# A key-choosing stage whose weight preparation moves from GpSimd to VectorE

## The chip, the core and the metric

The kernel runs on one core of one Trainium2 chip. The metric is the device time of one execution in microseconds (us). A core has five engines that work from queues of their own: TensorE (PE in the profile, its weight loads PEld), VectorE (DVE), ScalarE (ACT), GpSimd (POOL) and SyncE (SP, which here only issues transfers). They wait for each other through semaphores.

## The reference, cut to what matters

The program is two blocks of a network over 512 tokens of width 1024. The first block has four mixers; one of them attends only to chosen keys. Its choice, and the gated sum into which each mixer's result goes, are

```python
rel = jax.nn.relu(jnp.einsum('bqhd,bsd->bqhs', iqb, ik).astype(jnp.float32) * IDX_DIM ** -0.5)
score = jnp.einsum('bqhs,bqh->bqs', rel, iwb.astype(jnp.float32)) * IDX_HEADS ** -0.5
score = jnp.where(admissible[None], score, -jnp.inf)
_, idx = lax.top_k(score, keep)          # keep = 128 of 512
...
gates = jax.nn.sigmoid(p["gate"].reshape(bsz, seq, N_BRANCHES, D_MODEL))
merged = jnp.sum(gates * jnp.einsum('bsnc,ncd->bsnd', ys, w_branch[l]), axis=2)
```

## The kernel before, in words

The kernel is a row of stages, each a block with a barrier at its end: the next stage's first instructions start when every engine has finished the last one. Through most stages runs one *stream* of weight tiles (class `Stream`): while an engine works on the stage's own algorithm, the others push tiles of the big products through in between. A tile is 128 columns of a weight matrix, 128 x 1024 values in SBUF. It passes through these steps:

- SyncE loads it (`raw`, three slots of two tiles, `Stream.load`).
- ScalarE rounds it to the high half, `w_hi` (L1406, `Stream.round`). It may do so two tiles ahead: `w_hi` and `w_lo` have two buffers each.
- `Stream.rest` makes the low half, `w_lo = raw - w_hi` (L1430, one instruction over 128 x 1024 values). It counts up the semaphore `split`, for which TensorE waits.
- TensorE makes 24 matmuls into `acc` (L1476 to L1478), and, where the tile belongs to a gated sum, 4 more into `br` (L1486).
- ScalarE takes `tanh` of `acc` into `sg` (L1417), VectorE multiplies `sg` by `br` (L1439, `Stream.product`, semaphore `mixed`), and `Stream.sum` adds `sg` to `merged`, or copies it there where it is the first mixer's (L1448, semaphore `added`).

There is one buffer `br` only. So TensorE's four L1486 matmuls of a tile wait until the tile before has had its product. The waits of the other steps are the same in all stages:

```python
def dve(self, dve, n):
    if n == 0:
        self.rest(dve, self.nc.vector, 0)
    self.rest(dve, self.nc.vector, n + 1)
    if n:
        self.mix(dve, n - 1)        # product, then sum, both on VectorE
```

All stages but one call this `Stream.dve`. The exception is `selection_stage`. It streams nine tiles, `fill` (below f0 to f8): the eight of the first gated sum and the first one of the second. VectorE there searches the 128 largest scores of each of 128 queries, for three blocks of queries (i = 1, 2, 3, with 256, 384 and 512 keys). A block has

- a sum of eight heads: one L2324 and seven L2326 (`masks = rel * iw + masks`),
- 16 rounds, each a MAX8 (L2341) that finds the eight largest and a MATCH_REPLACE8 (L2342, with a short MATCH_VALUE_LOAD ahead of it) that takes them out,
- one L2344 that turns the result into a mask.

After every sixth of the 48 rounds, and once at the end, stands a *step* of the stream: steps 0 to 7 stand ahead of rounds 0, 6, 12, ... 42, step 8 behind the last round. In step s VectorE makes the product of tile f(s-1) (none in step 0, whose tile before has no gated sum). GpSimd meanwhile runs a loop of its own over the same nine tiles, `Stream.pool`: the low half of tile f(s+1) as soon as ScalarE has rounded it, then the sum of tile f(s-1) once its product is there. The order of each engine's work is the order in which the code issues it; no planner is in between.

Of the kernel before, what the change touches and what calls it, by code (L numbers as in the profile page):

```python
# [1031 lines left out]
def experts_by_token(c, table, x_dram, y_dram, w_gate, w_up, w_down, room_yg, room):  # L1032
# [5 lines left out]
    with ExitStack() as ctx:  # L1038
# [17 lines left out]
        with c.stage() as block:  # L1056
# [11 lines left out]

            @block.gpsimd
            def _(pool):  # L1070
                def index(dst, j, col, count):
                    nc.gpsimd.tensor_copy(dst, table[:, j, col:col + 1]).then_inc(idx_copied, 1)
# [239 lines left out]
class Stream:  # L1312
# [148 lines left out]
        if n:  # L1461
            self.mix(dve, n - 1)

    def pool(self, pool, n):
        self.rest(pool, self.nc.gpsimd, n + 1)
        self.sum(pool, self.nc.gpsimd, n - 1)

    def pe(self, pe, n):
        tile = self.tiles[n]
        pe.wait_ge(self.split, n + 1)  # L1470
# [756 lines left out]
def selection_stage(c, stream, fill, iq, small, ik, gain, lat, lat_t, iw, masks):  # L2227

    nc = c.nc
    with ExitStack() as ctx:
        rel, best = c.sb(ctx, "rel", [P, 8, S]), c.sb(ctx, "best", [P, 8])
        rows, sq, st = c.sb(ctx, "rows", [P, NT, P]), c.sb(ctx, "sq", [P, NT, 64]), c.sb(ctx, "st", [P, 3, NT, 1])
        ps, tps = c.ps(ctx, "rel_ps", [P, 4, 512]), c.ps(ctx, "turn_ps", [P, 512])
        ik_in, turned, rows_ready, var, rooted, lat_ready, dots, relu, used, chain = (c.sem(x) for x in (
            "ik_in", "turned", "rows", "var", "rooted", "lat", "dots", "relu", "used", "dve"))
        rounds, per = 3 * KEEP // 8, 6
        with c.stage() as block:
            @block.sync  # L2240
            def _(sp):
                for b in range(4):
                    sp.dma_start(ik[32 * b:32 * b + 32, :], small[64:96, :]).then_inc(ik_in, 16)
                for n in fill:
                    stream.load(sp, n + 2)

            @block.tensor
            def _(pe):
                def products(i):
                    pe.wait_ge(ik_in, 64)  # L2250
                    for h in range(8):
                        n = 8 * (i - 1) + h
                        if n >= 4:
                            pe.wait_ge(relu, n - 3)
                        b, wd = 32 * (h % 4), (i + 1) * P
                        pe.matmul(ps[:, n % 4, 0:wd], iq[b:b + 32, h // 4, i * P:(i + 1) * P], ik[b:b + 32, 0:wd],
                                  start=True, stop=True).then_inc(dots, 1)

                for i in range(NT):
                    mm = pe.transpose(tps[:, i * P:i * P + 120], small[0:120, i * P:(i + 1) * P], c.const("ident")[0:120, 0:120])  # L2260
                mm.then_inc(turned, 1)
                for s, n in enumerate(fill):
                    if s == 0:
                        products(1)
                    if s == 1:
                        products(2)
                    if s == 4:
                        products(3)
                    stream.pe(pe, n)
                    if s == 1:  # L2270
                        pe.wait_ge(lat_ready, 1)
                        for i in range(NT):
                            mm = pe.transpose(tps[:, i * P:(i + 1) * P], lat[:, i, :], c.const("ident"))
                        mm.then_inc(turned, 1)

            @block.scalar
            def _(act):
                def rectified(i):
                    for h in range(8):
                        n, wd = 8 * (i - 1) + h, (i + 1) * P  # L2280
                        act.wait_ge(dots, n + 1)
                        if n >= 8:
                            act.wait_ge(used, n - 7)
                        nc.scalar.activation(rel[:, h, 0:wd], ps[:, n % 4, 0:wd], ACT.Relu, scale=32 ** -0.5).then_inc(relu, 1)

                act.wait_ge(turned, 1)
                nc.scalar.copy(rows[:, :, 0:120], tps[:].rearrange("p (i d) -> p i d", i=NT)[:, :, 0:120]).then_inc(rows_ready, 1)
                for s, n in enumerate(fill):
                    stream.act(act, n)
                    if s == 0:  # L2290
                        rectified(1)
                        act.wait_ge(var, 1)
                        nc.scalar.activation(st[:, 1], st[:, 0], ACT.Sqrt).then_inc(rooted, 1)
                    if s == 1:
                        rectified(2)
                    if s == 2:
                        act.wait_ge(turned, 2)
                        nc.scalar.copy(lat_t, tps[:])
                    if s == 4:
                        rectified(3)  # L2300

            @block.gpsimd
            def _(pool):
                for n in fill:
                    stream.pool(pool, n)

            @block.vector
            def _(dve):
                run = Chain(dve, chain)
                dve.wait_ge(rows_ready, 1)  # L2310
                run(nc.vector.tensor_tensor(sq[:], rows[:, :, 0:64], rows[:, :, 0:64], ALU.mult))
                run(nc.vector.tensor_reduce(st[:, 0], sq[:], AX.X, ALU.add))
                run(nc.vector.tensor_scalar(st[:, 0], st[:, 0], 1.0 / 64, 1e-6, ALU.mult, ALU.add))
                dve.sem_inc(var, 1)
                run(nc.vector.tensor_scalar(iw, rows[:, :, 112:120], 8 ** -0.5, None, ALU.mult))
                taken = 0
                for i in range(1, NT):
                    wd = (i + 1) * P
                    m, d = masks[:, i - 1, 0:wd], masks[:, i - 1, i * P:wd]
                    for h in range(8):  # L2320
                        n = 8 * (i - 1) + h
                        dve.wait_ge(relu, n + 1)
                        if h == 0:
                            ins = nc.vector.tensor_scalar(m, rel[:, h, 0:wd], iw[:, i, 0:1], None, ALU.mult)  # L2324
                        else:
                            ins = nc.vector.scalar_tensor_tensor(m, rel[:, h, 0:wd], iw[:, i, h:h + 1], m, ALU.mult, ALU.add)  # L2326
                        ins.then_inc(used, 1)
                        dve.wait_ge(used, n + 1)
                    run(nc.vector.tensor_tensor(d, d, c.const("causal"), ALU.add))
                    if i == 1:  # L2330
                        dve.wait_ge(rooted, 1)
                        run(nc.vector.reciprocal(st[:, 2], st[:, 1]))
                        run(nc.vector.tensor_tensor(sq[:], rows[:, :, 0:64], st[:, 2].broadcast_to([P, NT, 64]), ALU.mult))
                        for r in range(2):
                            run(nc.vector.tensor_tensor(lat[:, :, 64 * r:64 * r + 64], sq[:],
                                                        gain.unsqueeze(1).broadcast_to([P, NT, 64]), ALU.mult))
                        dve.sem_inc(lat_ready, 1)
                    for _r in range(KEEP // 8):
                        if taken % per == 0:
                            stream.product(dve, fill[taken // per] - 1)  # L2340
                        run(nc.vector.max(best[:], m))  # L2341
                        run(nc.vector.match_replace(m, best[:], m, TAKEN))  # L2342
                        taken += 1
                    run(nc.vector.tensor_scalar(m, m, TAKEN / 1.5, NEG, ALU.is_ge, ALU.mult))  # L2344
                for n in fill[(rounds + per - 1) // per:]:
                    stream.product(dve, n - 1)


def gla_stage(c, stream, fill, q, k, vt, low, gate, a_up, a_bias, gain, lat, w_uv, th, y_lat, y):
# [489 lines left out]
```

## Time and profile before

| what | value |
|---|---|
| median of three runs | 2821.92 us (2821.71 to 2823.41) |
| the profiled execution, device time | 2821.36 us |
| its span, first to last instruction | 2819.6 us |
| PE, PEld, DVE, ACT, POOL busy | 2266.8, 1693.7, 1423.7, 854.0, 125.6 us |
| L1430 on DVE, all stages | x203, 248.0 us, mean 1224 ns |

In the tables of the profile a row names line, engine, operation and `output<-input`, then the shape of output and input. A busy time is the sum of instruction times on an engine. Instructions of one engine overlap a little: the next can start some hundredths of a microsecond before the last is through, so what an instruction costs in a row of them is the distance from its start to the next start. PEclk is the clock granted to TensorE as a share of its full speed: 1.00 is 2.4 GHz and 0.50 is 1.2 GHz.

### The profile page before, as it was taken

The page shows a single profiled execution, that of the slowest core. Times are in us where ns is not written, and L with a number is a line of the kernel's source. Part 1 is how long each engine was busy: PE and PEld are TensorE (multiplying, and loading weights), DVE is VectorE, ACT ScalarE, POOL GpSimd, SP SyncE. Part 2 cuts the span into 40 slices and gives each one's busy share as a digit, 9 for nine tenths or more (in the row PEclk, how much of TensorE's full clock was granted, in tenths as well). Part 3 has the DMA queues.
Part 4 walks back from the last instruction along what each step waited for, and adds up shares of the span by engine and source line. Part 5 has one row for each costly group of instructions (what it writes and reads, how often), then busy time and mean ns, then how long its engine had stood idle before and what let it go on. Part 6 is the DMA issues. An engine that isn't in the chain of part 4 may idle for free. (4 is left out here: it accounts for less than half of the span.)

```text
span 2819.6 us, 30685 instructions
## 1 busy us (share of the span) xinstructions
PE 2266.8 (80%) x11238; PEld 1693.7 (60%) x11238; DVE 1423.7 (50%) x2420; ACT 854.0 (30%) x1395; POOL 125.6 (4%) x161
## 2 busy tenths in 40 slices
PE   6345599899985299994259998999964998999986
PEld 4145476566764166763247766777754776687765
DVE  2272335866434266664434457584333445767333
ACT  2020133223221166652233323222222433232221
POOL 0000000200000122221000000000000000000000
PEclk9655599999996599997579999999987999999998
DMA  4100233122110599994233221223114331122311
GB/s 125 64 12 8 79 97 96 56 79 72 60 60 18 148 335 334 341 338 151 101 123 113 75 71 53 75 94 120 41 67 136 97 90 50 59 85 95 118 53 67
DMA packets 281413, 300.03 MB, mean 106 GB/s; under 512 B 58958, under 2 KB 253598, under 8 KB 281226
## 3 DMA queue, kind: packets, MB, share of 16 engines
q1 hardware_dynamic: 271786, 289.57, 31.9%
q0 software_dynamic: 9472, 8.43, 0.9%
q8 instruction: 94, 1.54, 0.2%
q14 instruction: 61, 0.49, 0.1%
HBM read 294.89 MB, written 33.19 MB: 116 GB/s over the span
## 5 line engine op out<-in xcount | busy, mean ns | idle before, releaser
L1476 PE MATMUL acc<-x_hi,w_hi 128*128 128x512 f32 x1632 | 679.7, 416 | 37.5 <-DVE w_lo L1430 32.5
L1478 PE MATMUL acc<-x_hi,w_lo 128*128 128x512 f32 x1632 | 644.3, 395 | 0.0
L1477 PE MATMUL acc<-x_lo,w_hi 128*128 128x512 f32 x1632 | 644.3, 395 | 0.0
L1406 ACT CAST w_hi<-raw 128x1024 fp32r<-128x1024 f32 x212 | 220.8, 1044 | 767.5 <-PE acc L1478 711.7
L1430 DVE TENSOR_TENSOR w_lo<-raw,w_hi 128x1024 fp32r<-128x1024 f32 x203 | 248.0, 1224 | 394.0 <-ACT w_hi L1406 389.9
L1476 PEld LDWEIGHTS acc<-x_hi,w_hi 128*128 128x128 f32 x1632 | 312.5, 192 | 123.5 <-DVE w_lo L1430 33.5
L1477 PEld LDWEIGHTS acc<-x_lo,w_hi 128*128 128x128 f32 x1632 | 312.3, 191 | 75.2 <-issue 13.9
L1478 PEld LDWEIGHTS acc<-x_hi,w_lo 128*128 128x128 f32 x1632 | 311.2, 191 | 68.5
L1486 PE MATMUL br<-y_t,raw_b 128*128 128x512 f32 x448 | 215.8, 605 | 20.2 <-DVE sg L1439 20.2
L1224 DVE TENSOR_TENSOR w_lo<-wgu,w_hi 128x1024 fp32r<-128x1024 f32 x128 | 151.1, 1220 | 117.8 <-ACT w_hi L1180 113.3
L1180 ACT CAST w_hi<-wgu 128x1024 fp32r<-128x1024 f32 x128 | 128.6, 1050 | 158.6 <-DMA wgu<-in_moe_w_up 152.2
L1486 PEld LDWEIGHTS br<-y_t,raw_b 128*128 128x128 f32 x448 | 85.2, 192 | 87.0 <-issue 78.9
L1143 PE MATMUL ps<-wd,y 128*128 128x512 f32 x256 | 115.3, 593 | 0.5 <-DVE y L1244 0.5
L1130 PE MATMUL ps<-w_hi,x_hi 128*128 128x512 f32 x256 | 103.8, 405 | 2.7 <-DVE x_lo L1218 1.7
L692 PE MATMUL ps<-w_hi,m_hi 128*128 128x512 f32 x192 | 77.8, 405 | 35.0 <-DVE w_lo L708 35.0
L1132 PE MATMUL ps<-w_hi,x_lo 128*128 128x512 f32 x256 | 101.2, 395 | 0.0
L1131 PE MATMUL ps<-w_lo,x_hi 128*128 128x512 f32 x256 | 100.8, 394 | 0.0
L1439 DVE SCALAR_TENSOR_TENSOR sg<-sg,br 128x512 f32<-128x512 f32 x112 | 76.4, 682 | 39.9 <-PE br L1486 36.7
L2131 DVE SCALAR_TENSOR_TENSOR y_t<-pad,w,y_t 128x512 f32<-128x512 f32 x120 | 90.1, 751 | 3.4
L1612 ACT ACTIVATE probs<-scores,stat 128x256 f32<-128x256 f32 (+3 forms) x96 | 51.8, 540 | 124.9 <-DVE stat L1573 124.9
L1621 ACT COPY probs_t<-t_ps 128x256 f32<-128x256 f32 (+3 forms) x96 | 38.9, 406 | 142.1 <-PE t_ps L1534 142.1
L1417 ACT ACTIVATE sg<-acc 128x512 f32<-128x512 f32 x112 | 66.2, 591 | 36.7 <-PE acc L1478 36.6
(486 smaller groups left out, 2877.3 us busy)
## 6 DMA issues: line engine op xcount, KB each, us to landing
raw<-in_w_in SPq DMA_DIRECT2D x61, 1024.0 KB, 5.5
raw<-in_w_gate SPq DMA_DIRECT2D x40, 1024.0 KB, 5.2
wgu<-in_moe_w_gate SPq DMA_DIRECT2D x32, 1024.0 KB, 10.2
wgu<-in_moe_w_up SPq DMA_DIRECT2D x32, 1024.0 KB, 13.3
wd<-in_moe_w_down SPq DMA_DIRECT2D x32, 1024.0 KB
raw_b<-in_w_branch SPq DMA_DIRECT2D x56, 256.0 KB, 2.8
y_t<-in_w_out SPq DMA_DIRECT2D x6, 2048.0 KB, 7.9
room<-in_x SPq DMA_DIRECT2D x2, 2048.0 KB, 8.5
```

What stands on the lines that cost most here:

```text
L1130: pe.matmul(ps[:, 0, :], x_hi[:, u, k, :], w_hi[:, k, :], start=(k == 0), stop=False)
L1131: pe.matmul(ps[:, 0, :], x_hi[:, u, k, :], w_lo[:, k, :], start=False, stop=False)
L1132: mm = pe.matmul(ps[:, 0, :], x_lo[:, u, k, :], w_hi[:, k, :], start=False, stop=(k == KT - 1))
L1143: mm = pe.matmul(ps[:, 1 + 2 * u + half, :], ht[:, u, m * P:(m + 1) * P], wd[:, j % SLOTS, m, half * 512:half * 512 + 512], start=(m == 0) ...
L1180: nc.scalar.copy(part(w_hi, p), part(wgu[:, j % SLOTS], p)).then_inc(w_rounded, 1)
L1224: nc.vector.tensor_tensor(part(w_lo, p), part(wgu[:, j % SLOTS], p), part(w_hi, p).bitcast(F32), ALU.subtract).then_inc(w_split, 1)
L1406: self.nc.scalar.copy(self.w_hi[:, n % 2], self.weights(n)).then_inc(self.rounded, 1)
L1430: eng.tensor_tensor(self.w_lo[:, n % 2], self.weights(n), self.w_hi[:, n % 2].bitcast(F32), ALU.subtract).then_inc(self.split, 1)
L1476: pe.matmul(acc, hi, tile.hi[:, k, :], start=(k == 0), stop=False)
L1477: pe.matmul(acc, hi, tile.lo[:, k, :], start=False, stop=False)
L1478: mm = pe.matmul(acc, lo, tile.hi[:, k, :], start=False, stop=(k == KT - 1))
L1486: mm = pe.matmul(self.br[:], self.raw_b[:, b % self.SLOTS, k, tile.at:tile.at + P], tile.row[:, k, :], start=(k == 0), stop=(k == 1))
```

## The change

`Stream.pool` and the GpSimd loop are gone. At each of the nine steps VectorE calls `Stream.dve`, which makes the low half of the next tile, the product of the last one, and its sum. What an engine other than these two does, and in which order, stays as it was.

```diff
-    def pool(self, pool, n):
-        self.rest(pool, self.nc.gpsimd, n + 1)
-        self.sum(pool, self.nc.gpsimd, n - 1)
...
-            @block.gpsimd
-            def _(pool):
-                for n in fill:
-                    stream.pool(pool, n)
...
                     for _r in range(KEEP // 8):
                         if taken % per == 0:
-                            stream.product(dve, fill[taken // per] - 1)
+                            stream.dve(dve, fill[taken // per])
                         run(nc.vector.max(best[:], m))
                         run(nc.vector.match_replace(m, best[:], m, TAKEN))
...
                 for n in fill[(rounds + per - 1) // per:]:
-                    stream.product(dve, n - 1)
+                    stream.dve(dve, n)
```

VectorE around step 1, between rounds 5 and 6 of the search, before (`sg` is the gate of a tile, `br` its mixer's product, `best` the eight largest of a round):

```order
L2342 MATCH_REPLACE masks<-best,masks 128x256
L2341 MAX best<-masks 128x8
L2342 MATCH_REPLACE masks<-best,masks 128x256
L1439 SCALAR_TENSOR_TENSOR sg<-sg,br 128x512
L2341 MAX best<-masks 128x8
L2342 MATCH_REPLACE masks<-best,masks 128x256
```

The same place on VectorE now (lines behind the removed ones have moved up by 4 to 10):

```order
L2332 MATCH_REPLACE masks<-best,masks 128x256
L2331 MAX best<-masks 128x8
L2332 MATCH_REPLACE masks<-best,masks 128x256
L1430 TENSOR_TENSOR w_lo<-raw,w_hi 128x1024
L1439 SCALAR_TENSOR_TENSOR sg<-sg,br 128x512
L1448 COPY merged<-sg 128x512
L2331 MAX best<-masks 128x8
L2332 MATCH_REPLACE masks<-best,masks 128x256
```

The low half of the next tile now stands ahead of the product, and the sum behind it. Step 0 has the low half alone.

VectorE at the end of the stage, before:

```order
L2341 MAX best<-masks 128x8
L2342 MATCH_REPLACE masks<-best,masks 128x512
L2344 TENSOR_SCALAR masks<-masks 128x512
L1439 SCALAR_TENSOR_TENSOR sg<-sg,br 128x512
L152 UNCONDITIONAL_BRANCH
L1699 UNCONDITIONAL_BRANCH
L1564 SCALAR_TENSOR_TENSOR scores<-s_ps,bias 128x128
```

And now, where the branch at L152 is again the stage's end:

```order
L2331 MAX best<-masks 128x8
L2332 MATCH_REPLACE masks<-best,masks 128x512
L2334 TENSOR_SCALAR masks<-masks 128x512
L1430 TENSOR_TENSOR w_lo<-raw,w_hi 128x1024
L1439 SCALAR_TENSOR_TENSOR sg<-sg,br 128x512
L1448 COPY merged<-sg 128x512
L152 UNCONDITIONAL_BRANCH
L1695 UNCONDITIONAL_BRANCH
L1560 SCALAR_TENSOR_TENSOR scores<-s_ps,bias 128x128
```

In step 8 too, the last product, for which TensorE's last four matmuls of the stage wait, has the low half of the next stage's first tile ahead of it.

## Rows read from the trace of the kernel before

**Rows 1.** The selection stage as one stretch: busy time of each engine.
```profile
479.40:580.10 100.70, 81.45 (x309) 55.12 (x308) 86.76 (x191) 27.31 (x47) 26.69 (x17) 0.90 0.18 55
```
**Rows 2.** Waits, 479 to 582 us: who waited for whom, total, times, longest.
```profile
PE br L1486 <- DVE sg L1439: 13.0, 3, 7.8
```
**Rows 3.** Groups of GpSimd, 479 to 582 us: busy us, mean ns, idle before.
```profile
L1430 POOL TENSOR_TENSOR w_lo<-raw,w_hi 128x1024 fp32r<-128x1024 f32 x9 | 21.9, 2436 | 515.4 <-ACT w_hi L1406 515.4
L1448 POOL COPY merged<-sg 128x512 f32<-128x512 f32 x8 | 4.9, 614 | 35.9 <-DVE sg L1439 35.9
```
**Rows 4.** Timeline of DVE in another stage: start us, duration us, instruction.
```profile
1621.22 1.22 DVE L1430 TENSOR_TENSOR w_lo<-raw,w_hi 128x1024 fp32r<-128x1024 f32 x1 [0.87 <-ACT w_hi L1406]
1622.36 0.68 DVE L1439 SCALAR_TENSOR_TENSOR sg<-sg,br 128x512 f32<-128x512 f32 x1
1623.08 0.43 DVE L1448 COPY merged<-sg 128x512 f32<-128x512 f32 x1
1623.42 0.42 DVE L1567 TENSOR_SCALAR scores<-s_ps 128x256 f32<-128x256 f32 x1
```
**Rows 5.** Timelines of DVE and ACT at the steps of the stage.
```profile
498.35 0.69 DVE L1439 SCALAR_TENSOR_TENSOR sg<-sg,br 128x512 f32<-128x512 f32 x1 [0.72 <-DVE masks L2342]
498.96 0.42 DVE L2341 MAX8 best<-masks 128x8 f32<-128x256 f32 x1
...
506.50 1.04 ACT L1406 CAST w_hi<-raw 128x1024 fp32r<-128x1024 f32 x1 [5.18 <-PE acc L1478]
508.27 0.69 DVE L1439 SCALAR_TENSOR_TENSOR sg<-sg,br 128x512 f32<-128x512 f32 x1 [3.45 <-PE br L1486]
...
566.87 0.69 DVE L1439 SCALAR_TENSOR_TENSOR sg<-sg,br 128x512 f32<-128x512 f32 x1
577.04 0.69 DVE L1439 SCALAR_TENSOR_TENSOR sg<-sg,br 128x512 f32<-128x512 f32 x1
```
**Rows 6.** L2326 in blocks 2 and 3: ns min/median/max; GpSimd's timeline at both places.
```profile
L2326 DVE SCALAR_TENSOR_TENSOR masks<-rel,iw,masks x7: 618/619/2635, 513.6 to 519.5; 128x384 f32<-128x384 f32 x7
515.27 2.50 POOL L1430 TENSOR_TENSOR w_lo<-raw,w_hi 128x1024 fp32r<-128x1024 f32 x1 [4.68 <-ACT w_hi L1406]
...
L2326 DVE SCALAR_TENSOR_TENSOR masks<-rel,iw,masks x7: 750/752/2774, 543.2 to 550.0; 128x512 f32<-128x512 f32 x7
544.21 2.82 POOL L1430 TENSOR_TENSOR w_lo<-raw,w_hi 128x1024 fp32r<-128x1024 f32 x1 [3.62 <-ACT w_hi L1406]
```
**Rows 7.** L2342 in blocks 1 and 3: ns min/median/max, first and last start.
```profile
L2342 DVE MATCH_REPLACE8 masks<-best,masks x16: 406/408/411, 492.3 to 512.4; 128x256 f32<-128x256 f32 x16
...
L2342 DVE MATCH_REPLACE8 masks<-best,masks x16: 675/676/680, 551.9 to 575.9; 128x512 f32<-128x512 f32 x16
```
**Rows 8.** Timeline of PE in the stage, at its end, and once later.
```profile
558.00 3.75 PE L1486 MATMUL br<-y_t,raw_b 128*128 128x512 f32 x4 [7.80 <-DVE sg L1439]
...
567.88 1.88 PE L1486 MATMUL br<-y_t,raw_b 128*128 128x512 f32 x4
569.19 0.80 PE L1476 MATMUL acc<-x_hi,w_hi 128*128 128x512 f32 x1
...
577.87 1.95 PE L1486 MATMUL br<-y_t,raw_b 128*128 128x512 f32 x4 [2.63 <-DVE sg L1439]
580.15 0.38 PE L1526 MATMUL s_ps<-lat_t,proj 64*128 64x128 f32 x2 [0.32 <-PEq L152]
...
2396.73 3.43 PE L1486 MATMUL br<-y_t,raw_b 128*128 128x512 f32 x4 [3.78 <-DVE sg L1439]
```
**Rows 9.** Stretches: length, busy PE, PEld, DVE, ACT, POOL; PEclk, DMA share, GB/s.
```profile
553.00:556.00 3.00, 0.00 (x0) 0.00 (x0) 2.86 (x7) 0.00 (x0) 0.00 (x0) 0.52 0.00 0
577.00:579.00 2.00, 1.13 (x3) 0.68 (x4) 0.69 (x2) 0.00 (x0) 0.61 (x1) 1.00 0.00 0
602.00:604.00 2.00, 2.00 (x6) 1.61 (x5) 1.95 (x3) 0.63 (x2) 0.00 (x0) 0.50 0.00 0
630.00:632.00 2.00, 2.00 (x7) 1.56 (x6) 1.93 (x4) 0.00 (x0) 0.00 (x0) 0.60 0.00 0
```

## The prediction

> **What bounds the kernel now.** I read the stage's stretch first, then who waited for whom in it, then GpSimd's groups, and last the timelines of VectorE and TensorE around the steps. The stretch from 479.4 to 580.1 us is the selection stage. VectorE is busy in 86.76 of its 100.70 us, TensorE in 81.45, GpSimd in 26.69 [rows 1]. The reader should see that VectorE is the limit, and that its real load is above 86.76: each round waits for the one before, and the small gaps of that count as idle. TensorE waits three times, 13.0 us in all, for VectorE's product L1439 [rows 2], and its last four matmuls start at 577.87, just after VectorE's last product ended at 577.04 + 0.69 = 577.73 [rows 5, 8]. The next stage's first matmul starts at 580.15, with a branch ahead of it [rows 8]: the barrier. So what VectorE adds ahead of its last product goes one for one into the time, less what VectorE now waits itself. GpSimd's 26.8 us of work [rows 3] are nowhere on that path.
>
> **The change part by part.**
>
> *Low halves and sums on VectorE.* The trace has this very triple on VectorE in another stage: L1430, L1439, L1448 start at 1621.22, 1622.36 and 1623.08, and the next instruction at 1623.42 [rows 4]. So a low half costs 1.14 us, and product and sum 0.72 + 0.34 = 1.06. A product alone costs 498.96 - 498.35 = 0.61 [rows 5]. A step thus grows by 1.14 ahead of its product, and by 1.06 - 0.61 = 0.45 from the product to the next round. Up to the last product there are 9 low halves and 7 sums: 9 x 1.14 + 7 x 0.45 = 10.26 + 3.15 = 13.41 us. The eighth sum, 0.45, stands behind the last product and beside TensorE's last four matmuls, so it costs nothing; were they gone it would cost its 0.45.
>
> *Waits of VectorE that take some of it.* In step 1 VectorE waited 0.72 us; in step 2, 3.45 us for TensorE's `br` [rows 5]. Both waits come early, when VectorE is less than one tile behind. Step 0 adds 1.14. Step 1's wait vanishes whole: the product moves from 498.35 by 1.14 + 1.14 - 0.72 = 1.56, the next round by 2.01. In step 2 the rounds ended at 508.27 - 3.45 = 504.82; now at 506.83. The low half needs ScalarE's rounding, over at 506.50 + 1.04 = 507.54, hence starts about 507.6, and the product follows at 508.75, against 508.27: 0.48 late. From then on `br` and the rounded tile are always there first. So 0.72 + (3.45 - 0.77) = 3.40 us are absorbed.
>
> *GpSimd's work gone from beside VectorE.* Of the seven L2326 of block 2 one takes 2635 ns where the median is 619, in block 3 one takes 2774 against 752. GpSimd has a low half there at 515.27 for 2.50 us and at 544.21 for 2.82 us, within both chains [rows 6]. No other of the 14 is long. I take both stalls as collisions that go with GpSimd's work: 2.02 + 2.02 = 4.04 us back, all on VectorE's chain. The bounds are 0 (the stalls have another cause) and, if half of the other GpSimd low halves cost VectorE something unseen, a little more; I take 4.04, since both rows show it. The rounds show nothing of the kind: L2342 stays within 406 to 411 ns in block 1 and 675 to 680 in block 3 [rows 7], though GpSimd worked beside them in both.
>
> Here the Trainium skill can be weighed ("SBUF — State Buffer", section "Who interferes with whom"): a VectorE instruction with two SBUF inputs excludes a GpSimd instruction that reads SBUF, and the loser stands still for the whole instruction. L2326 reads `rel` and `masks`, and fits. MATCH_REPLACE8 is written with two inputs as well, `best` and `masks`, and by a plain reading it should collide too, and the sum would turn into a gain of some 4 us (rival D). The trace does not agree: no L2342 is long.
>
> *Sum at the last product.* 13.41 - 3.40 - 4.04 = 5.97 us: it starts at 583.01, TensorE's last four matmuls at 577.87 + 5.97 = 583.84.
>
> *TensorE's clock at the stage's end.* In step 7 the product moves by 5.97 - 1.14 - 0.45 = 4.38, from 566.87 to 571.25 [rows 5], so it ends at 571.94. Tile f7's `br` matmuls started at 567.88 and f8's main matmuls 1.31 later, and these ended at 577.87 - 2.63 = 575.24, 6.05 after their start at 569.19 [rows 8]. Now they run from some 573.3 to 579.3, and TensorE is idle for 4.5 us until 583.84, where it was idle for 2.63. After 2.63 the clock stood at 1.00 [rows 9]. In the idle stretch of 7.80 it had fallen to 0.50 from about its fourth microsecond, and after it the four matmuls took 3.75 us, not 1.95; after an idle stretch of 3.78 us later in the kernel they took 3.43 [rows 8, 9]. With 4.5 I expect the slow clock. It costs at least 3.43 - 1.95 = 1.5 us, which the barrier passes on, and up to 2.6 if, as after 558.0, the clock stays at half for about 5.3 us of work. I take 2.0; the other end is 0 (clock kept).
>
> *What costs nothing.* The low half of f(s+1) is now made late in steps 1 to 7, but TensorE needs it only after `br` of f(s), which itself waits for the product of the same step; so it is always there first. The loads that wait for `split` start up to 13 us later, but with three slots each is wanted two groups (four tiles, over 28 us) later. GpSimd has nothing left in the stage and nobody waits for it.
>
> Sum: 5.97 + 2.0 = 8.0 us. Against the profiled execution that is 2821.36 + 8.0 = 2829.3; the median of the runs is 0.56 above it, so 2829.9.
>
> **The rivals.**
>
> *A. The clock is kept at the stage's end.* Everything else as above: +6.0, 2827.9 us. For it: the clock held through 2.63 us. Against: it had fallen after 3.78.
>
> *B. The slow L2326 are not GpSimd's doing.* Then 4.04 us do not come back, and the stage ends 10.0 us late, with the slow clock 12: 2831.9 to 2833.9 us. Against it is that both lie exactly under a GpSimd low half. A run of worse clocks in the next stage (below, in the other direction) would look alike in the total.
>
> *C. Not slower: the clock pays it back in the next stage.* That stage loses its clock twice for a few microseconds, PEclk 0.50 in 602 to 604 and 0.60 in 630 to 632 [rows 9], in the short idle moments of its attention units. Where the clock falls depends on how idle moments lie, and the shift moves them. A cold stretch of about 3.5 us costs 1.7 us of TensorE's time. If both vanish, 3.4 us come back; with the clock kept at the stage's end too, 6.0 - 3.4 = +2.6 remain: 2824.5 us, no measurable change. It decides from one of the two gone together with the clock kept: +4.3. Likewise two further cold stretches would give +11.4.
>
> *D. Faster: the rounds too were held up by GpSimd.* Six of its nine low halves lie beside rounds; at 2.02 us each, as in L2326, 12 us more come back: 8.0 - 12.1 = -4, 2817.8 us. Rows 7 speak plainly against it.
>
> **How the numbers follow.** About 0.2%, or 5.6 us, can be told from no change. Forecast (slow clock, 4.04 back) 0.50; A 0.27; B, or a worse clock later, 0.10; C 0.11; D and anything else that gains 0.02. Slower by over 0.2% (above 2827.6) holds nearly all of the forecast and B, and some 0.6 of A: 0.49 + 0.16 + 0.10 = 0.75; same 0.22, of A's lower part, C and a little of the forecast; faster 0.03. The range leaves out most of C, the top of B and D: 2826.0 to 2833.5.
>
> **What the profile will show.** VectorE should have 9 L1430 of about 1.23 us and 8 L1448 of 0.43 in the stage, and no GpSimd row there. No L2326 over 0.76 us. No wait ahead of step 1's product, and under 1 us ahead of step 2's low half. Products of steps 3 to 8 late by 0.0, 1.6, 3.2, 2.8, 4.4 and 6.0 us, the next stage's first matmul near 586.1 to 588. TensorE's wait before its last four matmuls near 4.5 us, with PEclk 0.50 behind it. I am wrong if an L2326 is still long, if VectorE waits in a late step, or if the next stage does not start later by what VectorE's last product is late.

## The result: 5.9 us slower, with the profile after

The changed kernel takes 2829.28 us, the median of 11 runs (2828.14 to 2833.34); the kernel before, over its own 11 runs, 2823.36 us (2821.41 to 2827.67). The ratio is 1.0023, 95% interval 1.0013 to 1.0032, that is 3.7 to 9.0 us slower. The profiled execution took 2830.9 us, its span 2829.1.

The selection stage after, as one stretch (length, busy PE, PEld, DVE, ACT, POOL, then PEclk, DMA share, GB/s; it answers to [rows 1]):

```profile
480.86:589.50 108.64, 84.08 (x309) 56.03 (x308) 94.46 (x208) 27.42 (x47) 0.00 (x0) 0.89 0.17 51
```

It is 7.94 us longer (100.70 before), VectorE is busy 7.70 us more, and GpSimd not at all. The stage also begins 1.45 us later than in the first profile, before anything that the change touches; six profiles of the two kernels place its first VectorE instruction anywhere from 481.29 to 483.70 us. I therefore count all times inside the stage from that instruction (481.29 us before, 482.74 after). From the next stage's first matmul to the span's end it is 2239.45 us before and 2239.55 after: in this pair of profiles nothing is given back or lost later. Between executions this remainder moves more: over all six profiles, three of each kernel, it lies between 2236.2 and 2239.6 us, with a mean of 2238.0 before and 2238.2 after.

The groups of VectorE in the stage (busy us, mean ns, idle before; to [rows 3, 6]):

```profile
L1430 DVE TENSOR_TENSOR w_lo<-raw,w_hi 128x1024 fp32r<-128x1024 f32 x9 | 11.0, 1225 | 1.6 <-ACT w_hi L1406 1.2 <-DVE lat L2325 0.2
...
L2316 DVE SCALAR_TENSOR_TENSOR masks<-rel,iw,masks 128x512 f32<-128x512 f32 x7 | 5.3, 752 | 0.2
...
L2316 DVE SCALAR_TENSOR_TENSOR masks<-rel,iw,masks 128x384 f32<-128x384 f32 x7 | 4.3, 619 | 0.2
L1448 DVE COPY merged<-sg 128x512 f32<-128x512 f32 x8 | 3.4, 427 | 0.3
```

The nine low halves and eight sums are there, 14.4 us busy. The head sums now have means of 619 and 752 ns, the old medians: both long ones are gone. Step 2 on VectorE's timeline, to [rows 4, 5]:

```profile
508.04 0.41 DVE L2332 MATCH_REPLACE8 masks<-best,masks 128x256 f32<-128x256 f32 x1
509.70 1.22 DVE L1430 TENSOR_TENSOR w_lo<-raw,w_hi 128x1024 fp32r<-128x1024 f32 x1 [1.25 <-ACT w_hi L1406]
510.84 0.68 DVE L1439 SCALAR_TENSOR_TENSOR sg<-sg,br 128x512 f32<-128x512 f32 x1
511.55 0.43 DVE L1448 COPY merged<-sg 128x512 f32<-128x512 f32 x1
511.90 0.42 DVE L2331 MAX8 best<-masks 128x8 f32<-128x256 f32 x1
```

The distances 1.14, 0.71 and 0.35 are those of the other stage. The wait of 1.25 us is for ScalarE's rounding; `br` is there when the product's turn comes. TensorE and VectorE at the stage's end (to [rows 5, 8]):

```profile
583.97 1.23 DVE L1430 TENSOR_TENSOR w_lo<-raw,w_hi 128x1024 fp32r<-128x1024 f32 x1
585.12 0.68 DVE L1439 SCALAR_TENSOR_TENSOR sg<-sg,br 128x512 f32<-128x512 f32 x1
```

```profile
585.94 3.29 PE L1482 MATMUL br<-y_t,raw_b 128*128 128x512 f32 x4 [4.32 <-DVE sg L1439]
589.55 0.61 PE L1522 MATMUL s_ps<-lat_t,proj 64*128 64x128 f32 x4 [0.32 <-PEq L152]
```

The last product starts at 585.12 - 482.74 = 102.38 us of the stage, before at 577.04 - 481.29 = 95.75: 6.63 later. The next stage's first matmul is at 106.81 against 98.86: 7.95 later. The clock around the last four matmuls (stretches as in [rows 9]):

```profile
583.00:586.00 3.00, 0.06 (x1) 0.09 (x1) 2.90 (x5) 0.00 (x0) 0.00 (x0) 1.00 0.00 0
586.00:588.00 2.00, 2.00 (x3) 0.88 (x4) 0.26 (x1) 0.00 (x0) 0.00 (x0) 0.60 0.00 0
```

Through most of the idle stretch of 4.32 us the clock still stands at 2.4 GHz, and it falls to 1.2 GHz just as the matmuls run: 3.29 us for the four, 1.95 before.

### The profile page after: what moved, and what is told of

It is laid out like the page before. It is cut to its first block and busy times, and to the rows that moved or that the text cites. A ratio compares the mean times of both kernels' runs of the same rounds, so it can differ in the third digit from the quotient of the medians.

```text
span 2829.1 us, 30691 instructions
## 1 busy us (share of the span) xinstructions
PE 2272.9 (80%) x11238; PEld 1697.7 (60%) x11238; DVE 1431.7 (51%) x2437; ACT 853.3 (30%) x1395; POOL 100.0 (4%) x144
## 5 line engine op out<-in xcount | busy, mean ns | idle before, releaser
L1430 DVE TENSOR_TENSOR w_lo<-raw,w_hi 128x1024 fp32r<-128x1024 f32 x212 | 259.0, 1224 | 394.8 <-ACT w_hi L1406 391.1
L1118 PE MATMUL ps<-consts,y 128*128 128x128 f32 x256 | 34.1, 277 | 54.2 <-DMA y<-x_scratch,gi 54.2
```

Of the source, the lines that this page charges most:

```text
L1430: eng.tensor_tensor(self.w_lo[:, n % 2], self.weights(n), self.w_hi[:, n % 2].bitcast(F32), ALU.subtract).then_inc(self.split, 1)
```

## The experiments

All of them change only the selection stage. The table counts in us from the stage's first VectorE instruction; "four" is the duration of TensorE's last four matmuls of the stage.

| kernel | last product | four | next stage's first matmul | runs |
|---|---|---|---|---|
| before, three profiles | 95.75, 96.16, 95.97 | 1.95, 3.43, 1.95 | 98.86, 100.75, 99.08 | 2823.36 |
| changed, three profiles | 102.38, 102.23, 101.82 | 3.29, 3.38, 3.59 | 106.81, 106.77, 106.56 | 2829.28 |
| low halves only | 99.24 | 3.35 | 103.74 | 2825.28 (1 run) |
| sums only | 101.25 | 2.89 | 105.30 | 2829.61 (1 run) |
| GpSimd waits | 92.02 | 3.65 | 96.82 | 2818.20 |
| product first | 101.49 | 3.22 | 105.86 | 2827.81 (1 run) |
| GpSimd work beside | 104.25 | 3.75 | 109.15 | 2833.94 (1 run) |
| TensorE kept busy | 102.25 | 1.96 | 105.36 | 2825.81 |
| waits, early product | 87.28 | 1.88 | 93.40 | 2816.17 |

### The two halves of the change, each alone

```diff
     def pool(self, pool, n):
-        self.rest(pool, self.nc.gpsimd, n + 1)
         self.sum(pool, self.nc.gpsimd, n - 1)
...
+                            stream.rest(dve, nc.vector, fill[taken // per] + 1)
                             stream.product(dve, fill[taken // per] - 1)
...
+                    stream.rest(dve, nc.vector, n + 1)
                     stream.product(dve, n - 1)
```

> VectorE makes the low halves in the nine steps, GpSimd keeps the sums. My theory adds its terms one by one: nine low halves of 1.14 us, less 3.4 us of VectorE's early waits (2.8 where the slow clock at the stage's start lasts as long as in the changed kernel), less 4.04 us for the two collisions, since GpSimd makes no low half any more: VectorE's last product 2.8 to 3.5 us later than before, counted from the stage's first VectorE instruction. No L2316-like head sum above 0.76 us. Rival (the two long head sums are not GpSimd's low halves' doing): they stay, and the product is 6.9 to 7.5 us late.

Measured: last product at 99.24, 3.49 us later than in the first profile of before, at the upper end of my interval, and 3.28 later than the mean of before's three; no long head sum (blocks of seven in 4.54 and 5.48 us, against 6.56 and 7.50). The rival fell.

The other half keeps GpSimd's low halves and gives the sums to VectorE:

```diff
     def pool(self, pool, n):
         self.rest(pool, self.nc.gpsimd, n + 1)
-        self.sum(pool, self.nc.gpsimd, n - 1)
...
-                            stream.product(dve, fill[taken // per] - 1)
+                            stream.mix(dve, fill[taken // per] - 1)
...
-                    stream.product(dve, n - 1)
+                    stream.mix(dve, n - 1)
```

> VectorE makes the sums, GpSimd keeps the low halves. My theory: 0.45 us for each sum, the first of them lost in the wait for br of step 2, so six count: last product 2.7 us late from the stage's start. The two long head sums (2.6 and 2.8 us against 0.62 and 0.75) stay, perhaps a little shorter where GpSimd starts first. Rival (the collisions come from GpSimd's sums, or from having any work there at all): they go, and the product is 1.3 us early.

A miss: the last product came 5.50 us late, not 2.7. The rival fell too, since both long head sums stayed. On VectorE's timeline of this kernel two of the eight sums are long; here is the first, and GpSimd's low half:

```profile
508.67 0.69 DVE L1439 SCALAR_TENSOR_TENSOR sg<-sg,br 128x512 f32<-128x512 f32 x1 [2.99 <-PE br L1485]
509.40 1.31 DVE L1448 COPY merged<-sg 128x512 f32<-128x512 f32 x1
```

```profile
508.03 2.40 POOL L1430 TENSOR_TENSOR w_lo<-raw,w_hi 128x1024 fp32r<-128x1024 f32 x1 [8.85 <-ACT w_hi L1406]
```

The copy, 427 ns alone, ends with GpSimd's subtraction, at 510.7 against 510.43. So a copy on VectorE collides as well: twice 0.88 us, 1.76 of the 2.8 missing. Another 0.76 is a wait of step 5 for TensorE's `br`, which had run late after an idle stretch of 3.94 us with the slow clock behind it, and 0.24 arose before step 2. The two halves alone lose 3.49 + 5.50 us, together 6.63: while GpSimd makes low halves, the sums cost more on VectorE than in the full change.

### GpSimd waits instead of colliding

```diff
-                for n in fill:
+                for s, n in enumerate(fill):
+                    if s in (3, 6):
+                        pool.wait_ge(used, 16 if s == 3 else 24)
                     stream.pool(pool, n)
```

> The kernel before, but GpSimd waits with the low halves of f4 and f7 until VectorE has summed the heads of blocks 2 and 3 (8 instructions each). Nothing is removed and nobody gets less work. My theory (GpSimd's low half stops a head sum of VectorE for its whole duration): both long head sums become 0.62 and 0.75 us, the last product comes 4.0 us earlier, the next stage's first matmul too, and the kernel takes 4.0 us less, ratio 0.9986. Rival (the head sums are long for a reason of their own, such as waiting for ScalarE's part): they stay long and the time is that of before.

Measured: 2818.20 us, median of 11 runs, against 2822.43 of before beside it; ratio 0.9985 (0.9976 to 0.9994). The last product is at 92.02, 3.73 to 4.14 us earlier than in the three profiles of before. VectorE's head sums of block 2, and GpSimd's low half, which now waits for them:

```profile
515.28 4.55 DVE L2328 SCALAR_TENSOR_TENSOR masks<-rel,iw,masks 128x384 f32<-128x384 f32 x7
```

```profile
519.91 2.51 POOL L1430 TENSOR_TENSOR w_lo<-raw,w_hi 128x1024 fp32r<-128x1024 f32 x1 [7.63 <-DVE masks L2328]
```

No work was removed: two instructions of 2.5 us moved by a few microseconds, and the stage became shorter by what the two collisions had cost. One part of the expectation failed in the profile: the next stage's first matmul, at 96.82, is only 2.04 us earlier than in the first profile of before (98.86), because the clock was slow at the last four matmuls here (3.65 us for the four, not 1.95).

### GpSimd work beside VectorE in the changed kernel

```diff
+            @block.gpsimd
+            def _(pool):
+                hi, lo = stream.tiles[fill[0]].hi[:, 0:2, :].bitcast(F32), stream.tiles[fill[0]].lo[:, 0:2, :].bitcast(F32)
+                pool.wait_ge(used, 2)
+                nc.gpsimd.tensor_tensor(junk[:], hi, lo, ALU.subtract).then_inc(junk_done, 1)
+                pool.wait_ge(used, 10)
...
+                nc.gpsimd.memset(junk[:], 0.0).then_inc(junk_done, 1)
+                pool.wait_ge(stream.mixed, 4)
...
+                nc.gpsimd.tensor_tensor(junk[:], hi, lo, ALU.subtract).then_inc(junk_done, 1)
+                pool.wait_ge(used, 18)
...
+                nc.gpsimd.tensor_copy(junk[:], hi).then_inc(junk_done, 1)
```

> The changed kernel, with four GpSimd instructions that serve nothing put beside VectorE: a subtraction of 128 x 1024 values with two SBUF inputs beside the head sums of block 1; a fill of the same size, which only writes, beside those of block 2; the same subtraction beside the rounds behind step 4; a copy of the same size beside the head sums of block 3. My theory (GpSimd's reads and a VectorE instruction with two SBUF tensors exclude each other): one head sum of block 1 takes about 2.5 us instead of 0.485, one of block 3 about 1 to 2.5 us instead of 0.75, and none of block 2 is long; MAX8 and MATCH_REPLACE8 stay as they are. Rival 1 (any GpSimd work stops it): one head sum of block 2 is longer by up to 1 us. Rival 2 (the long ones had nothing to do with GpSimd): no instruction changes.

The head sums of blocks 1, 2 and 3 (ns min/median/max), then MATCH_REPLACE8 between 521 and 546 us, and GpSimd's timeline:

```profile
L2332 DVE SCALAR_TENSOR_TENSOR masks<-rel,iw,masks x7: 485/485/2690, 487.2 to 492.5; 128x256 f32<-128x256 f32 x7
...
L2332 DVE SCALAR_TENSOR_TENSOR masks<-rel,iw,masks x7: 619/619/620, 517.2 to 521.1; 128x384 f32<-128x384 f32 x7
...
L2332 DVE SCALAR_TENSOR_TENSOR masks<-rel,iw,masks x7: 750/752/1626, 549.6 to 555.2; 128x512 f32<-128x512 f32 x7
...
L2348 DVE MATCH_REPLACE8 masks<-best,masks x14: 542/542/544, 522.8 to 543.4; 128x384 f32<-128x384 f32 x14
```

```profile
487.73 2.35 POOL L2302 TENSOR_TENSOR junk<-x_hi,x_lo 128x1024 f32<-128x1024 f32 x1 [487.26 <-DVE masks L2332]
517.90 0.95 POOL L2305 MEMSET junk<- 128x1024 f32 x1 [27.82 <-DVE masks L2332]
536.23 2.63 POOL L2308 TENSOR_TENSOR junk<-x_hi,x_lo 128x1024 f32<-128x1024 f32 x1 [17.37 <-DVE sg L1439]
550.45 1.06 POOL L2311 COPY junk<-x_hi 128x1024 f32<-128x1024 f32 x1 [11.59 <-DVE masks L2332]
```

The theory held in all four places. Beside a subtraction of 2.35 us one head sum grew by 2.20 us, beside a copy of 1.06 us one grew by 0.87, beside a fill of 0.95 us none (each case once, in one profile), and the rounds did not notice the second subtraction. The first collision is larger than the 2.02 us of the kernel before, where one takes 2635 ns against 619 [rows 6]. The last product is only 2.1 us later than the changed kernel's mean (104.25 against 102.14), because VectorE's wait of step 2 took up a part of the first collision. The write-only case is what the Trainium skill says ("SBUF — State Buffer", section "Who interferes with whom"): a VectorE instruction with two SBUF inputs is stopped by a GpSimd instruction that reads SBUF, not by one that only writes it; the trace agrees. For the rounds, another page of the Trainium skill resolves my plain reading of that rule. "VectorE: DVE Perf Modes", section "Two Vector instructions with no wait between them", counts MATCH_VALUE_LOAD and MATCH_REPLACE_8 as two instructions with one input each. The 542 to 544 ns above agree.

### The order within a step

```diff
-                            stream.dve(dve, fill[taken // per])
+                            stream.mix(dve, fill[taken // per] - 1)
+                            stream.rest(dve, nc.vector, fill[taken // per] + 1)
...
-                    stream.dve(dve, n)
+                    stream.mix(dve, n - 1)
+                    stream.rest(dve, nc.vector, n + 1)
```

> The changed kernel, with product and sum ahead of the low half in each step. My theory: the last product has no low half ahead of it, 1.14 us less; but in step 2 VectorE now waits for br with the low half still to do, about 0.6 us more. Last product 0.5 us earlier than in the changed kernel, TensorE's last idle stretch 3.2 to 3.8 us instead of 4.3. If the clock then holds, another 1.3 us at the next stage's start. Rival (the order in a step costs nothing, since TensorE is not waiting for the product but for the low half): the last four matmuls start as late as in the changed kernel.

Measured: last product at 101.49, 0.65 earlier than the mean of the changed kernel's three profiles (102.14), and the next stage 0.85 earlier than their mean (106.71). The last four matmuls start at 102.32 us, against 103.20, 103.06 and 102.65 in the changed kernel's three profiles, so the rival does not hold; but this is one profile, and it lies only 0.33 us outside the three. My number for TensorE's idle stretch was wrong: it is 4.32 us again, and the clock fell again (3.22 us for the four). f8's main matmuls follow the product of step 7, which also moved forward, so both ends of the stretch shift together.

### TensorE kept busy in its last idle stretch

```diff
+                    def warm():
+                        pe.wait_ge(relu, 24)
+                        hi = stream.tiles[n].hi
+                        for k in range(16):
+                            pe.matmul(ps[:, 0, :], hi[:, k % 8, 0:P], hi[:, k % 8, :], start=True, stop=True)
+
-                    stream.pe(pe, n)
+                    stream.pe(pe, n, warm if s == 8 else None)
```

> The changed kernel, with 16 matmuls that serve nothing (into a free bank, 0.23 us each) between f8's 24 main matmuls and its last four, where TensorE is idle for 4.3 us. My theory (the slow clock behind that idle stretch costs the stage's end 1.3 us): granted clock 1.00 at the last four matmuls, they take 1.95 us instead of 3.29, and the next stage's first matmul comes 1.3 us earlier from the stage's start. Rival (the slow clock comes from what was before, or the barrier hides it): the clock falls all the same, or the next stage starts no earlier.

TensorE's timeline at the stage's end, then the clock:

```profile
581.37 3.79 PE L2271 MATMUL rel_ps<-x_hi 128*128 128x512 f32 x16
585.87 1.96 PE L1484 MATMUL br<-y_t,raw_b 128*128 128x512 f32 x4 [0.71 <-DVE sg L1439]
588.15 0.49 PE L1524 MATMUL s_ps<-lat_t,proj 64*128 64x128 f32 x4 [0.32 <-PEq L152]
```

```profile
586.00:588.00 2.00, 1.82 (x4) 0.52 (x4) 0.18 (x1) 0.00 (x0) 0.00 (x0) 1.00 0.00 0
```

The last product is where it was (102.25), the four matmuls take 1.96 us, and the next stage starts at 105.36, 1.35 earlier than the changed kernel's mean. From the last product's start to the next stage's first matmul it takes 3.11 us here, as in the two profiles of before with the full clock; in the changed kernel's three it takes 4.43, 4.54 and 4.74. So the clock's share at the stage's end is 1.3 to 1.6 us. The runs lean the same way, 2825.81 us (median of 10) and 1.0013 (1.0004 to 1.0022) against before; that interval overlaps the changed kernel's, so by the runs alone the gain is not settled.

### Both kernels profiled again

> The kernel before once more, for a second profile. Two theories on the gap between the stage's shift in the first two profiles (7.95 us at the next stage's first matmul) and that of the medians (5.9 us). Theory 1: the clock at TensorE's last four matmuls of the stage is a matter of chance also in the kernel before, since it fell once behind an idle stretch of 2.73 us in the version with GpSimd's waits; some profiles of before then show it slow there, next stage up to 1.8 us later, with the last product at 95.6 to 96.1 us from the stage's first VectorE instruction in all. Theory 2: the VectorE chain itself varies from run to run by a microsecond or more.

> The changed kernel once more. Theory 1: last product again 102.1 to 102.6 us from the stage's first VectorE instruction, no long head sum, VectorE waiting 0.8 to 1.3 us in step 2; only the clock at the last four matmuls may differ (1.95 or 2.9 to 3.8 us for the four). Theory 2: the last product moves by a microsecond or more.

> As the other repetition of the kernel before. Theory 1: last product at 95.6 to 96.1 us, the clock at the stage's end full or half. Theory 2: the product elsewhere.

> As the other repetition of the changed kernel. Theory 1: last product at 102.1 to 102.6 us, the clock at the stage's end full or half. Theory 2: the product elsewhere.

The four took 2824.42, 2828.48, 2818.77 and 2829.59 us. The last product keeps within 0.41 us in three profiles of before, within 0.56 in three of the changed kernel; this last spread follows VectorE's wait in step 2 (1.25, 1.10 and 0.71 us), which the expectation's lower end of 0.8 missed. The clock is the looser part. In one of the three profiles of before it had fallen at the stage's end, although the idle stretch was no longer than in the others (2.45 us against 2.63 and 2.53):

```profile
580.65 3.43 PE L1486 MATMUL br<-y_t,raw_b 128*128 128x512 f32 x4 [2.45 <-DVE sg L1439]
```

On the means of three, the product moves by 102.14 - 95.96 = 6.18 us and the next stage's first matmul by 106.71 - 99.56 = 7.15. The medians of the runs moved by 5.92, with an interval that holds both. So theory 1 held, though two products lie outside the ranges that I gave: 96.16 us in before (95.6 to 96.1) and 101.82 in the changed kernel (102.1 to 102.6).

The next stage, which the change does not touch, has a spread of its own. From its first matmul to the first one behind its barrier it takes 92.68, 89.39 and 91.03 us in the three profiles of before, and 92.68, 92.57 and 89.41 in those of the changed kernel. Here are the first matmul behind it in the second profile of before and in the third of the changed kernel (the stage began at 584.40 and 589.05), and that third profile's clock where the first ones have a slow stretch:

```profile
673.79 1.09 PE L2386 MATMUL ps<-proj,a_up 16*128 16x512 f32 x2 [0.65 <-PEq L152]
```

```profile
678.46 1.09 PE L2376 MATMUL ps<-proj,a_up 16*128 16x512 f32 x2 [0.65 <-PEq L152]
```

```profile
611.00:613.00 2.00, 2.00 (x10) 1.64 (x10) 1.97 (x3) 0.51 (x2) 0.00 (x0) 1.00 0.00 0
637.00:639.00 2.00, 2.00 (x10) 1.66 (x9) 1.93 (x4) 0.00 (x0) 0.00 (x0) 1.00 0.00 1
```

The profiles of 92.6 to 92.7 us lose the clock twice in this stage, that of 91.0 once, those of 89.4 never; each time costs about 1.6 us.

### A version that beats both

```diff
 (with the two waits of GpSimd above)
                             stream.product(dve, fill[taken // per] - 1)
+                        if taken == rounds - 3:
+                            stream.product(dve, fill[8] - 1)
...
-                for n in fill[(rounds + per - 1) // per:]:
-                    stream.product(dve, n - 1)
```

> The version with GpSimd's two waits, and besides the last product moved from behind the search to three rounds before its end. Its inputs are there by then, and TensorE can run its last four matmuls right behind f8's main ones. My theory: beyond the 4.0 us of the waits, the stage's end comes 2.2 us earlier, when VectorE's last mask instruction ends and not TensorE's last matmul; TensorE has no idle stretch of over 1 us at the end; in all 6.2 us less than before, ratio 0.9978. Rival (VectorE's search ends last in any case and TensorE's tail is beside it): no gain beyond the version with the waits.

Measured: 2816.17 us, median of 11, ratio 0.9980 (0.9971 to 0.9989), 6.2 us under before's 2822.33 beside it. TensorE and VectorE at the stage's end:

```profile
573.23 1.88 PE L1486 MATMUL br<-y_t,raw_b 128*128 128x512 f32 x4
576.39 0.49 PE L1526 MATMUL s_ps<-lat_t,proj 64*128 64x128 f32 x4 [1.29 <-PEq L152]
```

```profile
575.43 0.43 DVE L2348 TENSOR_SCALAR masks<-masks 128x512 f32<-128x512 f32 x1
```

TensorE's four follow the main matmuls without an idle stretch, and the stage ends with VectorE's last mask at 575.86; TensorE has been through since 575.11, and its only wait at the end, 1.29 us, is the one for the next stage. The next stage begins at 93.40. That is 3.42 earlier than with the waits alone, 1.7 of which is the slow clock that this profile of the waits had (3.65 us for the four, not 1.95). The earlier product itself brings the other 1.7, where I expected 2.2; by the runs the second edit brings 2.0 us, but the two intervals overlap, so of the second edit only the profile is firm.

## Why the prediction was right

Forecast 2829.9 us, measured 2829.28; a shift of 8.0 forecast, 5.9 measured by the medians and 7.95 in the first pair of profiles. That the totals agree within 0.6 us is in part luck. The median of before came out at 2823.36 us, 1.4 above the 2821.92 that I had started from, and this made up for most of the 2.1 us by which the shift was forecast too large. In the first pair two errors of the sum cancel: the last product was 0.66 us later than forecast (6.63 against 5.97), and the slow clock cost 0.68 less (1.32 against 2.0). Point by point:

- *VectorE is the limit and the barrier passes its last product on.* Right. The stretch grew by 7.94 us, the next stage started later by it, and the rest of the program has the same mean in both kernels within 0.2 us.
- *13.41 us of added work.* Right: distances of 1.14, 0.71 and 0.35 us in step 2, nine low halves and eight sums.
- *3.40 us absorbed.* A little too much. The low half of step 2 waited 1.25, 1.10 and 0.71 us for the rounding in the three profiles, where I took 0.77. In the first of them TensorE stayed slow until about 494.3 us, 11.5 after the stage's first VectorE instruction, where it had been 10.3. So tile f0 and ScalarE's rounding behind it were late. In the first profile every product from there on is some 0.6 us later than I forecast: 0.7, 2.3, 3.9, 3.4, 5.0 and 6.6 us for steps 3 to 8 against 0.0, 1.6, 3.2, 2.8, 4.4 and 6.0. Part of this is a spread between executions that both kernels have: step 2's product lies between 26.98 and 27.39 us in the three profiles of before, and between 27.54 and 28.10 in the changed kernel's. On the means of three the last product moved by 6.18, near the 5.97 of the sum.
- *4.04 us back from the two collisions.* Right, and the best supported term: the long head sums went with the low halves (changed kernel, low halves only), stayed where GpSimd kept them (sums only), went when GpSimd only waited (4.2 us in the runs), and came back when work was put beside them. Rival B is refuted, and D with it: no round was ever held up.
- *The slow clock at the stage's end, 2.0 us.* Right in kind for this kernel: it fell in all three profiles, so rival A (the clock kept) did not come about in any. As to size, keeping TensorE busy gave back 1.35 us, and its share is 1.3 to 1.6, so I took 0.4 to 0.7 too much. What I did not see is that the kernel before pays this price in some executions too: my argument from the length of the idle stretch (2.63 us kept, 3.78 us lost) was too sharp. The clock fell behind 2.45 and 2.73 us here, and in the changed kernel it was still full after most of 4.3 us. The means of three moved less than the first pair (7.15 us against 7.95): 0.35 of this lies in the clock (0.97 for 1.32), which before paid for in one of its three, and 0.45 the last product's own spread. What lies between these 7.15 and the 5.92 of the medians is inside the interval of the runs, and its cause is not shown; how often before pays for the slow clock, three profiles do not say.
- *Rival C.* In the first profile after, the next stage lost its clock twice again (PEclk 0.58 in 610 to 612 us, 0.50 in 638 to 640), so nothing was paid back there:

```profile
610.00:612.00 2.00, 1.69 (x5) 1.41 (x6) 0.98 (x3) 2.00 (x5) 0.00 (x0) 0.58 0.03 8
638.00:640.00 2.00, 2.00 (x6) 1.61 (x5) 1.63 (x2) 1.17 (x3) 0.00 (x0) 0.50 0.59 206
```

But both slow stretches were gone in the third profile of the changed kernel, and in the second of before. So what C counts on, up to 3.3 us from this stage, does come about, in some executions of either kernel; that the change makes it more or less likely, no run shows. That the first profiles agreed in this stage to the hundredth (92.68 us) is luck.

## What to carry to other kernels

An engine that works off the critical path can still cost the one on it: look for single instructions that take far more than their group's median, and see what GpSimd runs at that moment. If it is a collision, try moving the off-path instruction before you move the work: here a wait on GpSimd gained 4.2 us, where taking the work from it lost 5.9. And count a stage's times from its own first instruction; the drift of earlier stages between executions (2.4 us here) and the spread of the next one (3.3 us) are each about half of the 5.9 us that this change costs.

## What the runs showed of the hardware

- VectorE's 427 ns copy of 128 x 512 values took 1.31 us when it came up while GpSimd subtracted. I had forecast collisions for two-input instructions only, and this copy has one.
- A one-input VectorE instruction over only 128 x 32 values, the scaling of `iw` at the stage's start, took 2132 ns beside GpSimd's first low half and 181 without it. Its end was hidden: VectorE then waits 3.0 us for ScalarE, where it had waited 1.0 in the kernel before.
- TensorE's clock at one and the same place of one and the same program differs from execution to execution, behind idle stretches within 0.2 us of each other. In a stage that no edit touched it fell twice, once or never, and the stage took 92.6 to 92.7, 91.0 or 89.4 us.
- Where a head sum was stopped, GpSimd's own low half was longer too: 2.50 and 2.82 us [rows 6], against 2.34 to 2.41 for its other seven in the stage. Why, no run was made to show.
